# First tile of x in two token halves, second weight unit's products by operand parts, and the last product's first weight unit summed in DRAM and split ahead

## What is computed

```
h = rms_norm(x, norm_mix_pre)
z = h @ w_in                      # ten blocks of 1024 columns; s_v is one of them
merged = three gated branches (short convolution, convolution of 31 taps, spatial gating)
x = x + rms_norm(merged @ w_out, norm_mix_post)
h = rms_norm(x, norm_ffn_pre)
f = square(relu(h @ w_ff1)) @ w_ff2       # w_ff1: 1024 x 4096, w_ff2: 4096 x 1024
x = x + rms_norm(f, norm_ffn_post)
```

## Time and profile before

| | us |
|---|---|
| median of 3 runs | 953.14 |
| lowest and highest | 953.08, 953.18 |
| the profiled execution | 953.15 |
| its span in the trace | 951.4 |
| PE busy | 942.5 (99%) |
| DVE busy | 718.6 (76%) |
| ACT busy | 431.8 (45%) |

### The profile page before, as it was taken

How to read it: one execution, slowest core, us unless ns; L and a number is a source line. 1 busy time by engine, 2 the same in 40 slices (tenths; PEclk the granted TensorE clock), 3 DMA queues, 4 the chain that set the end, 5 groups by cost and what they waited for, 6 DMA issues and landing times.

```text
span 951.4 us, 13451 instructions
## 1 busy us (share of the span) xinstructions
PE 942.5 (99%) x4824; PEld 807.5 (85%) x4824; DVE 718.6 (76%) x844; ACT 431.8 (45%) x536; POOL 102.9 (11%) x135
## 2 busy tenths in 40 slices
PE   9999999999999999999999999999999999999997
PEld 7888888888888888888888888899889989989985
DVE  5579879888888988886584444599975875786698
ACT  6543333333333322224374323377745745754774
POOL 1211001001100012222200000120001001100100
PEclk9999999999999999999999999999999999999999
DMA  8447558656755724454477323538586756848664
GB/s 319 141 160 229 172 169 229 186 189 193 196 187 176 199 89 132 132 134 153 134 194 248 111 89 112 198 129 236 167 253 133 235 171 154 229 133 244 187 191 132
DMA packets 41228, 168.01 MB, mean 177 GB/s; under 512 B 4953, under 2 KB 5089, under 8 KB 38881
## 3 DMA queue, kind: packets, MB, share of 16 engines
q1 hardware_dynamic: 31872, 111.85, 32.5%
q0 software_dynamic: 7680, 35.13, 20.8%
q10 hardware_dynamic: 1632, 20.45, 5.8%
HBM read 163.22 MB, written 37.75 MB: 211 GB/s over the span
## 4 chain that ended last, share of the span: by engine, by line
PE 97%; DVE 1%; DMA 1%; issue 0%; ACT 0%; SPq 0%; DVEq 0%
PE ps L1621 26%; PE ps L1625 26%; PE ps L1623 26%; PE ps L1816 6%; PE ps L1818 6%; PE ps L1820 6%; PE ps L1751 1%; DMA glu<-xt_in 1%; PE ps L1666 0%; DVE w_lo L1101 0%; DVE wide L1480 0%; DVE end L1468 0%; DVE wide L1463 0%; ACT c_hi L737 0%; DVE end_a L1468 0%
## 5 line engine op out<-in xcount | busy, mean ns | idle before, releaser
L1101 DVE TENSOR_TENSOR w_lo<-raw,w_hi 128x1024 fp32r<-128x1024 f32 (+1 forms) x141 | 172.3, 1227 | 93.8 <-ACT w_hi L699 93.5
L699 ACT ACTIVATE w_hi<-raw 128x1024 fp32r<-128x1024 f32 (+1 forms) x140 | 146.1, 1052 | 202.2 <-PE ps L1625 118.3
L1621 PE MATMUL ps<-a_hi,w_hi 128*128 128x512 f32 x576 | 224.9, 390 | 0.0
L1625 PE MATMUL ps<-a_hi,w_lo 128*128 128x512 f32 x576 | 224.2, 389 | 0.0
L1623 PE MATMUL ps<-a_lo,w_hi 128*128 128x512 f32 x576 | 224.1, 389 | 0.0
L1189 DVE SCALAR_TENSOR_TENSOR conf<-glu,cols,conf (+1 forms) x240 | 186.8, 778 | 27.5 <-DVE conf L1189 26.4
L1625 PEld LDWEIGHTS ps<-a_hi,w_lo 128*128 128x128 f32 x576 | 108.1, 188 | 22.6
L1623 PEld LDWEIGHTS ps<-a_lo,w_hi 128*128 128x128 f32 x576 | 108.2, 188 | 22.2
L1621 PEld LDWEIGHTS ps<-a_hi,w_hi 128*128 128x128 f32 x576 | 108.2, 188 | 22.2
L1621 PE MATMUL ps<-w_hi,h_hi 128*128 128x512 f32 x224 | 87.2, 389 | 0.0
L1623 PE MATMUL ps<-w_lo,h_hi 128*128 128x512 f32 x224 | 87.2, 389 | 0.0
(11 more groups left out here) (186 smaller groups left out, 1580.4 us busy)
## 6 DMA issues: line engine op xcount, KB each, us to landing
raw<-units_in SPq DMA_DIRECT2D x127, 512.0 KB, 3.3
weight_sums<-units_in POOLq DMA_DIRECT2D x16, 1024.0 KB, 7.8
raw_v<-units_in SPq DMA_DIRECT2D x16, 512.0 KB, 6.0
glu<-units_in SPq DMA_DIRECT2D x16, 512.0 KB, 7.5
raw<-weight_sums SPq DMA_DIRECT2D x16, 512.0 KB, 4.2
glu<-units_in POOLq DMA_DIRECT2D x16, 512.0 KB, 5.3
raw_d<-units_in POOLq DMA_DIRECT2D x16, 512.0 KB, 6.5
glu<-weight_sums SPq DMA_DIRECT2D x8, 512.0 KB, 5.5
```

What stands on the lines that cost most here:

```text
L699: return nc.scalar.activation(dst, src, ACT.Copy, scale=scale)
L1101: return nc.vector.tensor_tensor(dst, src, hi, ALU.subtract)
L1621: nc.tensor.matmul(ps[:, bank, :], left_hi, right_hi, start=first, stop=False, skip_group_check=on_top)
L1625: return nc.tensor.matmul(ps[:, bank, :], left_lo, right_hi, start=False, stop=final, skip_group_check=on_top)
```

## The change

Three edits, in the listing below (the buffer's gain column now lies at column 0; all other uses of `xt` follow that and are left out):

- **The start.** k tile 0 of x is loaded in two DMAs, the gain with the first 256 tokens and then the other 256, and ACT makes its c_hi in two pieces. `WARM` is 9. PE waits for the first piece, and for the second ahead of its third matmul. Unit 1 goes by operand parts as unit 0 does.
- **The early unit.** `EARLY` is the unit h = 0 of product 4 in the last down part. POOL makes its sum of four blocks in DRAM (three DMAs of 512 KB, one behind each of three sums that it makes anyway), SP loads it into slot 4, ACT and DVE split it during the last up part into a buffer of its own. The accumulating DMA for it in slot 8 falls away, and its two splits from among the work of the end.
- **The end.** `weigh` of tile 0's second half moves to the end of product 7; `weigh` of tile 1's second half moves ahead of the last tile.

```diff
-WARM = 10
+WARM = 9
+FIRST = 1 + 2 * P
...
+EARLY = UNITS - 2
+EARLY_SUM = MATRICES * MADE_UNITS
+EARLY_SLOT = 4
+EARLY_BLOCKS = ((1, 0), (1, 1))
...
-    made_d = nc.dram_tensor("weight_sums", (MATRICES * MADE_UNITS, P, D), F32, kind="Internal").ap()
+    made_d = nc.dram_tensor("weight_sums", (MATRICES * MADE_UNITS + 1, P, D), F32, kind="Internal").ap()
...
+        xt_all = glu_flat[:, 0:KT * (SEQ + 1)].rearrange("p (k t) -> p k t", k=KT)
+        xt = xt_all[:, :, 1:]
...
+        early_w_hi, early_w_lo = resident(a_hi, 1), resident(a_lo, 1)
...
                     ff_load(q, DOWN, product)
+                    if q == QUARTERS - 1 and product == 1:
+                        sp.wait_ge(early_summed, 48)
+                        sp.wait_ge(w_lo_ready, ff_unit(q, UP, 4, 0) + 1)
+                        sp.dma_start(slots[EARLY_SLOT], made_d[EARLY_SUM]).then_inc(early_loaded, 16)
...
+            def early_step(n):
+                into = made_d[EARLY_SUM]
+                if n == 0:
+                    pool.dma_start(into, units_d[block_of(EARLY, EARLY_BLOCKS[0])]).then_inc(early_summed, 16)
+                elif n == 1:
+                    pool.wait_ge(early_summed, 16)
+                    pool.dma_start(into, units_d[block_of(EARLY, EARLY_BLOCKS[1])], accum_op=ALU.add,
+                                   max_dma_last_dim=SUM_BYTES).then_inc(early_summed, 16)
+                elif n == 2:
+                    pool.wait_ge(early_summed, 32)
+                    pool.wait_ge(made[5], 16 * MATRICES)
+                    pool.dma_start(into, made_d[(MATRICES - 1) * MADE_UNITS], accum_op=ALU.add,
+                                   max_dma_last_dim=SUM_BYTES).then_inc(early_summed, 16)
...
             for m in range(KT // 2, MATRICES):
                 pool.wait_ge(unit_done, U_GATE + 2 * (KT + m) + 2)
                 second_block(m, 7)
+                early_step(m - KT // 2)
...
-                    add_block(q, f, 4)
+                    add_block(q, f, 4, (1,) if (q, f) == (QUARTERS - 1, DOWN) else (0, 1))
...
-                copy_hi(w_hi[:, u % RING, :] if into is None else into, slots[slot]).then_inc(w_hi_ready, 1)
+                copy_hi(w_hi[:, u % RING, :] if into is None else into, slots[slot]
+                        ).then_inc(w_hi_ready, 2 if u == EARLY + 1 else 1)
...
-            act.dma_start(xt[:, 0, :], xt_d[0]).then_inc(xt_loaded[0], 16)
-            act.dma_start(xt[:, 1, :], xt_d[1]).then_inc(xt_loaded[1], 16)
+            act.dma_start(xt_all[:, 0, 0:FIRST], xt_d[0, :, 0:FIRST]).then_inc(first_loaded, 16)
+            act.dma_start(xt_all[:, 0, FIRST:], xt_d[0, :, FIRST:]).then_inc(xt_loaded[0], 16)
+            act.dma_start(xt_all[:, 1, :], xt_d[1]).then_inc(xt_loaded[1], 16)
...
-            gain_hi(0)
+            act.wait_ge(first_loaded, 16)
+            nc.scalar.activation(c_hi[:, 0, 0:2 * P], xt[:, 0, 0:2 * P], ACT.Copy,
+                                 scale=xt_all[:, 0, 0:1]).then_inc(first_hi, 1)
+            act.wait_ge(xt_loaded[0], 16)
+            nc.scalar.activation(c_hi[:, 0, 2 * P:], xt[:, 0, 2 * P:], ACT.Copy,
+                                 scale=xt_all[:, 0, 0:1]).then_inc(gained_hi, 1)
             act.wait_ge(raw_loaded[0], 16)
             copy_hi(w_hi[:, 0, HALF:], raw[:, 0, HALF:]).then_inc(w_hi_ready, 1)
...
             def split_behind(q, f, product, h):
                 u = ff_unit(q, f, product, h) + RING
-                if u < UNITS:
+                if u < UNITS and u != EARLY:
                     ff_hi(u)
...
                 for h in range(2):
                     done(q, UP, 7, h)
                     split_behind(q, UP, 7, h)
+                    if q == QUARTERS - 1 and h == 0:
+                        act.wait_ge(early_loaded, 16)
+                        copy_hi(early_w_hi, slots[EARLY_SLOT]).then_inc(early_hi, 1)
                 act.wait_ge(hidden_diff, 4 * q + 1)
                 set_hi(q, "22-21")
...
                 split_behind(q, UP, 7, 1)
                 set_lo(q, "22-21")
+                if q == QUARTERS - 1:
+                    dve.wait_ge(early_hi, 1)
+                    lo(early_w_lo, slots[EARLY_SLOT], early_w_hi).then_inc(early_lo, 1)
                 set_lo(q, "11")
...
                     if q == QUARTERS - 1 and product == 4:
                         dve.wait_ge(mlp_sum, sums_after(q, product, 0))
                         weigh(0, 0)
-                        weigh(0, 1)
+                        weigh(1, 1)
                         dve.wait_ge(out_weighted, 6)
                         finish(2, (0,))
...
                     elif product == 7:
                         finish(1)
+                        dve.wait_ge(mlp_sum, sums_after(q, product, 1))
+                        weigh(0, 1)
                     elif product == 4:
-                        weigh(1, 1)
                         dve.wait_ge(mlp_sum, sums_after(q, product, 1))
                         weigh(1, 0)
...
-            def unit_0(left, right, k, start=False):
-                w = slice(k * HALF, (k + 1) * HALF)
+            def by_parts(left, right, u, n, start=False, halfway=None):
+                w = slice(n * HALF, (n + 1) * HALF)
                 for c in range(CH):
-                    mm = nc.tensor.matmul(ps[:, c, :], left[:, k, c * P:(c + 1) * P], right[:, 0, w],
+                    if c == CH // 2 and halfway:
+                        halfway()
+                    mm = nc.tensor.matmul(ps[:, c, :], left[:, 2 * u + n, c * P:(c + 1) * P], right[:, u, w],
                                           start=start, stop=False)
                 return mm
-            for k in range(2):
-                pe.wait_ge(gained_hi, k + 1)
-                if k == 0:
-                    pe.wait_ge(half_hi, 1)
-                else:
-                    pe.wait_ge(w_hi_ready, 1)
-                unit_0(c_hi, w_hi, k, k == 0)
-                if k == 0:
-                    pe.wait_ge(half_lo, 1)
-                else:
-                    ready(Count(U_V))
-                unit_0(c_hi, w_lo, k)
-                pe.wait_ge(gained_lo, k + 1)
-                mm = unit_0(c_lo, w_hi, k)
-            mm.then_inc(unit_done, 1)
+            def first_units(u):
+                for n in range(2):
+                    first = u == 0 and n == 0
+                    if first:
+                        pe.wait_ge(half_hi, 1)
+                        pe.wait_ge(first_hi, 1)
+                    else:
+                        pe.wait_ge(w_hi_ready, u + 1)
+                        pe.wait_ge(gained_hi, 2 * u + n + 1)
+                    by_parts(c_hi, w_hi, u, n, first, (lambda: pe.wait_ge(gained_hi, 1)) if first else None)
+                    if first:
+                        pe.wait_ge(half_lo, 1)
+                    else:
+                        ready(Count(U_V + u))
+                    by_parts(c_hi, w_lo, u, n)
+                    pe.wait_ge(gained_lo, 2 * u + n + 1)
+                    mm = by_parts(c_lo, w_hi, u, n)
+                mm.then_inc(unit_done, 1)
+            for u in range(2):
+                first_units(u)
...
+                    unit_hi, unit_lo = ((early_w_hi, early_w_lo) if u == EARLY else
+                                        (w_hi[:, u % RING, :], w_lo[:, u % RING, :]))
                     mm = products(down_bank(q, product) + t, hi[:, k, at], low[:, k, at],
-                                  w_hi[:, u % RING, w], w_lo[:, u % RING, w], k == 0 and not again,
+                                  unit_hi[:, w], unit_lo[:, w], k == 0 and not again,
...
-                        ready(Count(ff_unit(q, DOWN, product, h)))
+                        u = ff_unit(q, DOWN, product, h)
+                        if u == EARLY:
+                            pe.wait_ge(early_lo, 1)
+                        else:
+                            ready(Count(u))
```

29 lines of the change are left out of this document (17 added, 12 removed).

## The result

The changed kernel takes **954.66 us** (median of 13 runs, 953.62 to 957.75) against 953.19 (13 runs, 953.08 to 953.57) in the same call: 1.0021 times, 95% interval 1.0013 to 1.0028. The forecast was 952.05, its range ended at 952.9. The sign is wrong, by a mechanism that the prediction had costed at nothing. The profiled execution took 954.55 (span 952.8), 1.4 more than that of before (953.15, span 951.4).

A forecast was written before the change was run, and what follows sets the result against it. PE was taken as the bound, with the chain on it for 97% of the span. The start's 0.33 and the end's 0.77 were subtracted: 953.15 - 0.33 - 0.77 = 952.05 us, range 951.5 to 952.9.

The forecast's parts named there:

- The early sums "cost at nothing": Gate products: three 512 KB DMAs on POOL, each behind a 1 MB sum that costs PE no wait, cost nothing.
- The early load: Last up part: issued at 894.35, landed at 898.9 as raw_v's load did, ahead of ACT's need at 899.6, so free.
- the rival's mechanism: Last up part: early load takes 9.0 us, ACT goes on late, PE stands 3.1 us; 955.2 in total, chance 0.04.
- the 0.6 that I took as covered: Ahead of down product 2: 0.6 us of early-load lateness is covered by DVE's slack, each further one costs fully.
- the later loads cannot hold up the early one: Last up part: one queue's descriptors are consumed in ring order, so the burst's later loads cannot delay the early load.
- The start: Up to spread in unit 3: smaller first load and no stall ahead of unit 1 give 0.33 after the root's limit.
- The stall's 0.48: Ahead of unit 1: PE's wait on w_lo, 0.40 plus 0.08 for an uncovered weight load, goes whole.
- the third issue delays k tile 1, needed only near 9: hidden: Start: ACT's third DMA issue, some 0.4 us, delays k tile 1, whose c_hi is needed only near 9; no cost.
- The cap: At spread: POOL's root stays at 25.57, so PE, some 0.7 early, waits and keeps only 0.33.
- The end: Behind PE's last matmul: an earlier last addition and fewer weighs behind it give 0.77, bounds 0.5 and 0.95.
- its two terms: End: last addition 0.28 earlier, at 944.58, and 0.49 saved behind it by one weigh less.
- Clock rising later: Unit 0: with one warm-up matmul less, pace stays at 0.43, costing 4.0; 955.7 in total, chance 0.03.

The follow-up runs named there:

- sums_only: The kernel before plus only the three early sums at the changed kernel's places, their results read by nothing: 955.09 us, 1.0027.
- third_there: The changed kernel with early sums one and two moved to the quiet part before the gate stage, the third left at 485 us: 956.16 us, 1.0027.
- third_later: The changed kernel with only the third early sum moved, behind the last 1 MB sum at 496 us: 952.70 us, 0.9995.
- start_only: The kernel before with the new start alone and the old order of weigh: 953.48 us, 1.0002.
- start_end: The changed kernel without the early unit (no early sums, no early load): 953.27 us, 0.9999.
- parts_only: The kernel before with only unit 1 by operand parts, x's first tile loaded whole and ten warm-up products: 952.54 us, 0.9996.
- late_load: best with the early load issued behind the loads of products 2 and 3 of the last down part: 956.63 us, 1.0038.
- early_old_weigh: best with the old order of weigh, the early unit kept: 952.68 us, 0.9994.
- third_there_2: The same kernel as third_there, one more profiled execution: 954.57 us.
- best: The changed kernel with its early sums in the quiet part (416 to 437 us), x's k tile 0 loaded whole, ten warm-up matmuls: 952.03 us, 0.9987.
- third_there_3: The same kernel as third_there, a further single profiled execution: 956.18 us.

## Why the prediction was wrong, step by step

- **The early sums "cost at nothing": this step failed,** for 1.98 us. I took from the earlier trace rows that the 1 MB sums of today cost PE no wait, and from that that half as much again would not either. No wait says nothing of slack. The matmul at 503.84, 0.50 long and 0.28 behind the one ahead of it, showed that b_lo was just in time, and I had not read the gate stage at all. sums_only shows the sums as the cause, third_there and third_later the third sum alone.
- **The early load: the rival's mechanism was right, its threshold was not.** It landed 6.1 us after the issue, not the 4.5 that I took, and the row of 6.2 in the very same place had been read as a moment (898.9) instead of a duration. Of the 0.6 that I took as covered beyond 5.3, some 0.1 was there: it costs in full from 5.4 on. I had compared with the first w_lo of down product 2 alone, but DVE is busy for 14.78 of the 15 us from 915 to 930 in the kernel before, so a shift of its list comes back at the units that follow. Measured +0.75. That the time, 954.66, lies near this rival's 955.2 is luck: most of the loss came from the sums. That the later loads cannot hold up the early one was drawn from the order of the ring alone; no run leaves them out, so it stays open.
- **The start: -0.33 forecast, -0.45 in the profile, nothing in the medians** of start_only and start_end. The stall's 0.48 did go. The step "the third issue delays k tile 1, needed only near 9: hidden" failed: it arrived at 8.3 instead of by 7.0. The root did not stay at 25.57 either: in the changed kernel it ended at 24.95, 0.67 before spread, and in all profiles at 24.70 to 26.67. The cap as such is real: in four profiles (parts_only, late_load, early_old_weigh, third_there_2) spread starts 0.14 to 0.15 behind the root, for 0.08 to 0.19 of loss. In the changed kernel PE came too late to meet it. Two errors against each other, so that the start's number is near by luck.
- **The end: right.** -0.77 forecast, -0.88 measured. With best and early_old_weigh its two terms come out apart as 0.28 (forecast 0.28) and 0.60 (0.49).
- **Clock rising later: did not happen** at the start. It can fall behind the new wait instead, as the trace of third_there_3 shows; in four of the changed kernel's 13 executions time and mean clock (0.996 to 0.997) fit that. That the three runs of before lay 0.1 us apart said nothing on the moment of the rise, since w_lo held unit 1 at about 12.35 in any case.
- **The chances:** 0.75 on the sum of two small gains, and 0.04 on a rival with the right shape (a late load behind which an in-order engine stands) but in only one of the places where DMA traffic was added.
